# A hybrid decoder step: cached K pages turned in blocks of 32 on VectorE, scored in 4x4 tiles of TensorE

## The chip, the core and the metric

The kernel runs on one core of a Trainium2 chip, as one launch. The metric is device time in microseconds, from the first to the last instruction with what lies around them, and lower is better. Five engines work in parallel, each through its own queue of instructions in program order: TensorE (PE; its weight loads are listed apart as PEld), VectorE (DVE), ScalarE (ACT), GpSimd (POOL) and SyncE (SP), which here issues nearly all transfers. They meet on semaphores: a name after "waits" below is the semaphore that an instruction waits for.

## What is computed

The program is one step of a two-layer decoder trunk for 512 prompt tokens and for 8 sample sequences of 4 new tokens each. A layer has an input projection, an HGRN2 recurrence and differential attention side by side (4 heads each, width 128), an output projection, and a mixture of 16 experts. What matters here is the attention of the sample sequences over a paged cache of 2048 earlier tokens, 16 pages of 128 each, whose numbers come from a page table:

```python
k_past = cache_k[l][page_table].reshape(bd, past_len, DA_HEADS, 2, DA_DK)
v_past = cache_v[l][page_table].reshape(bd, past_len, DA_HEADS, DA_DV)
# diff_attn_core, segments: past, then the new tokens
s = jnp.einsum('bqhcd,bkhcd->bhcqk', q, k).astype(jnp.float32) * scale
scores.append(jnp.where(kpos[None, :] <= qpos[:, None], s, NEG))
p = jax.nn.softmax(jnp.concatenate(scores, axis=-1), axis=-1)
a = p[:, :, 0] - lam * p[:, :, 1]
outs.append(jnp.einsum('bhqk,bkhd->bqhd', a[..., off:off + nk], v.astype(jnp.float32)))
```

Each head has two queries and two keys of 64 (c = 0, 1), so a sequence has 4 heads x 2 maps x 4 tokens = 32 score rows against 2048 keys. A page of K or V is 128 tokens x 512 numbers in fp32, 256 KB; a layer reads 128 pages of each. The sequences are called batches in the code, four pages a quad.

## The kernel before

In each layer the work around the change is one stage of SLOTS = 139 slots. It follows the prompt's attention and ends with the sample's last value product; then come the output projection, the routing and the experts. In every slot each engine's program places what belongs to that slot, so that the slots set the order on each queue: one cached page per slot on PE and ACT, with one item of the HGRN2 recurrence at every slot 5k//3, and the four blocks of the prompt's attention output at slots 2 to 5. The items are the recurrence's levels (PE L901 to L922, DVE L1536 to L1545) and then its blocks; the last eight are the steps of the sample states (POOL L1967 loads a state, DVE L1616 brings it up to date, POOL L1972 and L1974 store it).

A K page arrives with its 128 tokens on the partitions, and the scores need its 512 numbers there. So PE turns each page, four transposes of 128x128 against the identity into one PSUM bank (L744, two banks in alternation), and ACT copies the bank to one of two buffers of a quad (L1311). When a quad is turned, four products of 32 padded query rows with 512 keys follow, one for each head, each on its own 32 columns of the array (L755). A product in fp32 shows as two records in the profile, as x8 for four.

DVE brings the scores of a quad to SBUF with their maximum (L1574). After a batch's four quads come the maximum, four exponentials and one for the new tokens (ACT L1318), then five rounds: p is turned by PE (L777, L779), copied by ACT (L1326, L1328), and multiplied with the quad's V pages (L794, 16 products; L798 for the new tokens). The rows are then divided by their sum (DVE L1597), turned (L806) and written out (L1603, L1604). This happens for each of the eight batches while the next batch's pages are turned.

The transfers of the pages are all issued by SP, at L564: a quad of K, then a quad of V one quad behind. Before each quad SP reads four page numbers (L560) and checks their bounds. K lies in a ring of 8 pages and a load waits for PE's turn of the page it replaces; V lies in a ring of 5 quads and a load waits for the product that used the quad. The pages' room belongs to weights in the other stages, so the first loads of a layer wait for the input projection, and the output projection's weights (L530) wait for the last pages.

## Time and profile before

| | us |
|---|---|
| median of three runs | 1842.38 (1838.37 to 1847.37) |
| profiled execution, its own time | 1847.27 |
| its span, first to last instruction | 1845.6 |
| PE busy in the span | 1664.3 (90%) |
| DVE busy | 550.0 (30%) |
| ACT busy | 485.5 (26%) |
| POOL busy | 161.6 (9%) |

The shares are means over stages that differ much. In the page's 40 slices of the span the DMA share is 0.9 or more in the stages of the experts and of the cached pages, and 0.2 or less in the prompt's attention. The table is thus read as a first look; the stage itself is read in windows, in the groups of its lines and in the timeline.

### The profile page before, as it was taken

Reading aid. Unit: us, or ns where it says so; the run is one execution under the profiler, and the core shown is the slowest. Engines: PE = TensorE matmul, PEld = TensorE weight load, DVE = VectorE, ACT = ScalarE, POOL = GpSimd, SP = SyncE. Lnnn points to the kernel's source line nnn. Section 1 sums busy time; section 2 is a strip of 40 time slices with the busy share of each in tenths; the row PEclk is TensorE's granted clock in tenths of the full one; section 3 lists DMA queues with packets and bytes.
Section 4 is the critical chain, followed back from the end, with each engine's and each line's share of the span. In section 5 each row is a group of like instructions: output and inputs, shape, how many; then the busy total and the mean of one; then the engine's idle time right before and its main releaser. Section 6 shows DMA issues by size and latency. Waiting matters only on the chain. (4 is left out here: it accounts for less than half of the span.)

```text
span 1845.6 us, 32355 instructions
## 1 busy us (share of the span) xinstructions
PE 1664.3 (90%) x12442; PEld 923.6 (50%) x12442; DVE 550.0 (30%) x1522; ACT 485.5 (26%) x1038; POOL 161.6 (9%) x218
## 2 busy tenths in 40 slices
PE   6999998888799999999599999898988999999990
PEld 3457786665445433333244777666744453333330
DVE  2214536434312500000231155453432142000004
ACT  2112335664411011111110233446543110111111
POOL 1000003200100000000200000121010000000002
PEclk9999999999899999999799999999988979999995
DMA  8431009898860699899642200588987309989974
GB/s 259 159 115 46 24 25 330 292 330 284 281 245 32 239 396 411 342 411 411 230 164 81 75 30 24 173 295 309 323 279 276 147 20 385 408 340 411 411 306 168
DMA packets 172364, 437.69 MB, mean 237 GB/s; under 512 B 23921, under 2 KB 23922, under 8 KB 172210
## 3 DMA queue, kind: packets, MB, share of 16 engines
q1 hardware_dynamic: 155650, 377.26, 55.6%
q0 software_dynamic: 16560, 58.34, 8.4%
q8 instruction: 102, 1.67, 0.4%
q14 instruction: 52, 0.43, 0.1%
HBM read 402.91 MB, written 32.64 MB: 236 GB/s over the span
## 5 line engine op out<-in xcount | busy, mean ns | idle before, releaser
L993 PE MATMUL bank<-wslots,heads 128*32 128x512 f32 (+2 forms) x1088 | 266.0, 593 | 8.0 <-DMA hgrn<-in_w_up 4.3
L693 PE MATMUL bank<-xT,wslots 128*128 128x272 f32 x1024 | 241.8, 393 | 1.5 <-ACT heads L1261 0.8
L693 PEld LDWEIGHTS bank<-xT,wslots 128*128 128x128 f32 x1024 | 191.6, 190 | 40.7 <-issue 3.2
L993 PE MATMUL bank<-hgrn,heads 128*32 128x512 f32 (+2 forms) x704 | 182.8, 593 | 0.0
L647 PE MATMUL bank<-wslots,xT 128*128 128x512 f32 x384 | 174.4, 608 | 6.0 <-DMA wslots<-in_w_in 4.3
L744 PE MATMUL bank<-cst,wslots 128*128 128x128 f32 x1024 | 161.8, 286 | 17.5 <-ACT wslots L1311 6.5
L1864 DVE TENSOR_TENSOR temps<-temps,bank 128x512 f32<-128x512 f32 x24 | 16.5, 688 | 449.7 <-PE bank L993 449.7
L993 PEld LDWEIGHTS bank<-wslots,heads 128*32 128x32 f32 (+2 forms) x1088 | 85.2, 127 | 117.5 <-issue 112.9
L1017 PE MATMUL bank<-wslots,temps 128*32 128x512 f32 (+2 forms) x544 | 141.3, 594 | 1.4 <-ACT temps L1352 1.4
L744 PEld LDWEIGHTS bank<-cst,wslots 128*128 128x128 f32 x1024 | 114.3, 143 | 45.5 <-issue 39.2
L647 PEld LDWEIGHTS bank<-wslots,xT 128*128 128x128 f32 x384 | 72.9, 195 | 95.0 <-issue 90.4
L944 PE MATMUL bank<-wslots,xT 128*128 128x512 f32 x256 | 116.3, 615 | 3.8 <-DVE xT L1626 3.8
L1311 ACT ACTIVATE heads<-bank 128x512 f32<-128x512 f32 x128 | 74.5, 594 | 99.6 <-PE bank L744 99.3
L1311 ACT ACTIVATE wslots<-bank 128x512 f32<-128x512 f32 x128 | 75.8, 594 | 82.7 <-PE bank L744 82.7
L993 PEld LDWEIGHTS bank<-hgrn,heads 128*32 128x32 f32 (+2 forms) x704 | 55.2, 122 | 76.9 <-issue 76.9
L944 PEld LDWEIGHTS bank<-wslots,xT 128*128 128x128 f32 x256 | 50.1, 198 | 67.3 <-issue 63.1
L1347 ACT ACTIVATE heads<-bank 128x512 f32<-128x512 f32 x24 | 14.3, 597 | 249.8 <-PE bank L1017 249.8
L1574 DVE TENSOR_SCALAR_CACHE_REDUCE heads<-bank 128x512 f32<-128x512 f32 x64 | 44.2, 691 | 117.9 <-PE bank L755 105.2
L794 PE MATMUL bank<-wslots,heads 128*32 128x128 f32 x2048 | 74.8, 291 | 3.8 <-ACT heads L1326 3.8
L794 PEld LDWEIGHTS bank<-wslots,heads 128*32 128x32 f32 x2048 | 59.8, 117 | 31.8 <-ACT heads L1326 18.0
L1178 ACT ACTIVATE temps<-hid 128x1024 f32<-128x1024 f32 (+1 forms) x25 | 26.4, 1055 | 176.7 <-DVE hid L1848 125.0
L1017 PEld LDWEIGHTS bank<-wslots,temps 128*32 128x32 f32 (+2 forms) x544 | 43.6, 129 | 48.3 <-issue 45.8
(321 smaller groups left out, 2016.3 us busy)
## 6 DMA issues: line engine op xcount, KB each, us to landing
wslots<-in_cache_k SPq DMA_DIRECT2D x256, 256.0 KB, 4.4
wslots<-in_cache_v SPq DMA_DIRECT2D x256, 256.0 KB, 4.5
wslots<-in_w_gate SPq DMA_DIRECT2D x20, 2048.0 KB, 16.1
wslots<-in_w_down SPq DMA_DIRECT2D x20, 2048.0 KB, 15.0
wslots<-in_w_up SPq DMA_DIRECT2D x18, 2048.0 KB, 16.1
wslots<-in_w_in SPq DMA_DIRECT2D x14, 2048.0 KB, 10.3
hgrn<-in_w_up SPq DMA_DIRECT2D x10, 2048.0 KB, 20.3
hgrn<-in_w_gate SPq DMA_DIRECT2D x10, 2048.0 KB, 15.5
```

What stands on the lines that cost most here:

```text
L647: x = mm(bank[2 + m % 2][:, :], xT[:, c, tok(i)], w[:, c, :], start=(c == 0), stop=(c == DC - 1))
L693: x = mm(bank[6 + g % 2][:, 0:HALF], w[:, c, h * P:(h + 1) * P], xT[:, c, half * HALF:(half + 1) * HALF], start=(c == 0), stop=(c == DC - 1))
L744: x = tr(bank[s % 2][:, h * P:(h + 1) * P], kpage[s % NK][:, h, :], ident)
L794: x = mm(bank[5][32 * h:32 * h + 32, 0:HD], ptq[par][:, j, 32 * h:32 * h + 32], vquad[v % NV][:, j, h, :], start=(q == 0 and j == 0), stop ...
L944: x = mm(bank[2 + s][:, :], oT[:, c, tok(i)], w[:, c, :], start=(c == 0), stop=(c == DC - 1))
L993: x = mm(bank[2 + k][a:z, :], xeT[T_ % 2][:, c, a:z], weights((what, l, e), DC)[:, c, :], start=(c == 0), stop=(c == DC - 1))
L1017: x = mm(bank[5 + n][a:z, :], hT[T_ % 2][:, c, a:z], weights(("down", l, e), 4)[:, c, n * WB:(n + 1) * WB], start=(c == 0), stop=(c == 3))
L1178: link(A(junk[0:r, :], hid[0:r, i, :], ACT.Square, accum_out=ssq[0:r, i:i + 1]))
L1311: A(ktb[s // 4 % 2][:, s % 4].rearrange("p h n -> p (h n)"), bank[s % 2][:, :], ACT.Copy).then_inc(kt_ok, 1)
L1347: A(yt[b][:, 0:WB], bank[5][:, :], ACT.Copy).then_inc(y_ok, 1)
L1574: tell(V.tensor_scalar(scr[G_ % 6], bank[2][:, :], 1.0, None, ALU.mult, ALU.max, accum_out=mx5[:, g % 4:g % 4 + 1]), sq_ok)
L1864: link(V.tensor_tensor(hgt, silu[T_ % 2], bank[3][:, :], ALU.mult), hg_ok)
```

## The change

K pages are no longer turned whole. DVE transposes two pages with one instruction in place, by blocks of 32x32 (`turn_pages`, 64 a layer); after that each block has 32 of the 512 numbers on its partitions. The scores of a batch then run over all 16 pages at once: `batch_scores` has four steps d, one for each block of 32 numbers of a head, and each step has 16 products of 32x32 against 512 keys, one for each row group a and head h of the array. The four steps add up in four PSUM banks, one for each row group. Four batches share these banks: each has eight of the 32 rows (the padded queries put it there), so four batches share one round of score output, exponentials, turns of p and division (two groups a layer instead of eight batches).

K lies in three units of eight pages in slots 1 to 3, of which 24 pages are loaded ahead of the stage, and V in three quads. SP follows a list (`page_order`): 24 K pages and a V quad ahead, two V quads after the last projection weights; then four K quads after the scores of each batch, with V quads sorted between by their slots. The bounds checks of the page numbers are gone, and their read follows the wait. The slots' tables are new: scores at 13n to 13n + 3, the DVE's turns between, values for the first four batches at slots 51 to 88 and for the second four at 103 to 133. The first eight turns stand ahead of the division of the prompt's attention output on DVE. The first level of the recurrence on PE waits for that output's copy (`od_ok`). Smaller edits: the causal mask of the prompt's attention is made of `tri` by one operation, queries are spread to four row groups by 16 copies (`spread_queries`), and the logits are cleared after the stage.

```diff
+GB = 4
+GROUPS = DB // GB
+UNIT = 8
+NU = 3
+SCORE_BANKS = (0, 1, 2, 4)
...
-        kpage = [w_a[:, 4096 + 512 * s:4096 + 512 * (s + 1)].rearrange("p (h n) -> p h n", h=H) for s in range(8)]
-        vquad = [w_a[:, o:o + 2048].rearrange("p (j h n) -> p j h n", j=4, h=H) for o in (8192, 10240, 12288, 0, 2048)]
-        NK, NV = len(kpage), len(vquad)
+        kring = w_a[:, 4096:16384].rearrange("p (u g x) -> p u g x", u=NU, g=UNIT)
+        vquad = [a.rearrange("p (j h n) -> p j h n", j=4, h=H) for a in (t_a[:, 4096:6144], w_a[:, 0:2048], w_a[:, 2048:4096])]
+        NV = len(vquad)
...
-        ktb = [a.rearrange("p (j h n) -> p j h n", j=4, h=H) for a in (w_a[:, 14336:16384], t_a[:, 0:2048])]
-        scr = [t_a[:, 2048 + 512 * i:2560 + 512 * i] for i in range(6)]
-        ptq = [t_a[:, 5120 + 512 * i:5632 + 512 * i].rearrange("p (j n) -> p j n", j=4) for i in range(2)]
+        scr = t_a[:, 0:2048]
+        scr_out = scr.rearrange("p (g a k) -> p a g k", g=NPG, a=4)
+        ptq = t_a[:, 2048:4096].rearrange("p (g n) -> p g n", g=NPG)
+        on = t_a[:, 2048:2560]
...
-        def turns(b):
-            return (3, 5, 7, 9, 11) if b < DB - 1 else (3, 4, 5, 6, 7)
+        SLOTS = DB * NPG + 11
+        SCORES = [13 * n for n in range(DB)]
+        TURN_AT = {SCORES[n - 1] + d: 8 * n + x for n in range(1, DB) for x, d in enumerate((1, 3, 5, 7, 9, 10, 11, 12))}
+        SUM_UP = [SCORES[GB * g + GB - 1] + 4 for g in range(GROUPS)]
+        VALUES = [SUM_UP[0] + 8 + 5 * k // 2 for k in range(16)] + [SUM_UP[1] + 8 + 2 * k for k in range(16)]
+        NEW_AT = (8, SUM_UP[1] - 2)
+        ROWS_AT = (VALUES[15] + 2, VALUES[31] + 1)
...
+        def page_order():
+            late = [(SCORES[(q // 2 - NU) // 2] + 4, 0, q) for q in range(2 * NU, NQ)]
+            late += [(VALUES[v - NV] + 1, 1, v) for v in range(NV, NQ)]
+            early = [(0, 0, q) for q in range(2 * NU)] + [(0, 1, v) for v in range(NV)]
+            return early + sorted(late)
...
+                    for _, kind, q in page_order():
+                        if kind == 0:
+                            n, first_page = unit_pages(q // 2)
+                            slot, _count = k_fill(l, q)
+                            if q < 2 * NU:
+                                sp.wait_ge(*last_use(("in", l, 3 + q // 2)))
                             else:
-                                sp.wait_ge(pv_ps, vn(v - NV) + 1)
+                                sp.wait_ge(sq_ps, DB * l + (q // 2 - NU) // 2 + 1)
+                            ids = four_pages((NPG * n + first_page) // 4 + q % 2)
                             for j in range(4):
-                                load_page(previous[j], vquad[v % NV][:, j], t_in["cache_v"], vl[v % NV])
-                    sp.wait_ge(kt_ps, (l + 1) * DB * NPG)
+                                load_page(ids[j], kring[:, unit_of(q // 2), 4 * (q % 2) + j, :], t_in["cache_k"], kl[slot])
+                        else:
+                            if q == 0:
+                                sp.wait_ge(pa_pv, 16 * (l + 1))
+                                sp.wait_ge(st_v, 16 * NT * (l + 1))
+                            elif q < NV:
+                                sp.wait_ge(*last_use(("in", l, 6)))
+                            else:
+                                sp.wait_ge(pv_ps, vn(l, q - NV))
+                            ids = four_pages(q)
+                            for j in range(4):
+                                load_page(ids[j], vquad[q % NV][:, j].rearrange("p h n -> p (h n)"), t_in["cache_v"], vl[q % NV])
...
-            def page_turn(l, s):
-                g = l * DB * NPG + s
-                pe.wait_ge(kl[s % NK], 16 * (int(s % NK < NT) + l * (DB * NPG // NK) + s // NK + 1))
-                if g >= 2:
-                    pe.wait_ge(kt_ok, g - 1)
+            def batch_scores(l, n, d):
+                i, B = n % GB, l * DB + n
+                if d == 0:
+                    pe.wait_ge(kt_ok, 8 * B + 8)
+                    pe.wait_ge(qp_ok, B + 1)
+                    if i == 0:
+                        pe.wait_ge(sq_ok, 4 * (B // GB))
+                u, z = sorted((unit_of(2 * n), unit_of(2 * n + 1)))
                 for h in range(H):
-                    x = tr(bank[s % 2][:, h * P:(h + 1) * P], kpage[s % NK][:, h, :], ident)
-                x.then_inc(kt_ps, 1)
-            def quad_scores(l, g):
-                G_ = l * NQ + g
-                Q = qn(G_)
-                pe.wait_ge(kt_ok, 4 * G_ + 4)
-                pe.wait_ge(qz_ok, G_ // 4 + 1)
-                pe.wait_ge(sq_ok, Q)
+                    q0 = 24 - 8 * i + 32 * (H * d + h)
+                    c0 = h * HD + 32 * d
+                    for a in range(4):
+                        r = slice(32 * a, 32 * a + 32)
+                        x = mm(bank[SCORE_BANKS[a]][32 * h:32 * h + 32, :], qp[r, q0:q0 + 32], kring[r, u:z + 1:z - u, :, c0:c0 + 32],
+                               start=(i == 0 and d == 0), stop=(i == GB - 1 and d == 3))
+                if d == 3:
+                    x.then_inc(sq_ps, 1)
...
+            def new_values(l, g):
+                G = GROUPS * l + g
+                pe.wait_ge(pt_ok, 5 * G + 5)
+                for h in range(H):
+                    x = mm(bank[5][32 * h:32 * h + 32, :], ptn[0:NS, 32 * h:32 * h + 32],
+                           vtok[0:NS, PT, h * HD:(h + 1) * HD].unsqueeze(1).to_broadcast([NS, GB, HD]), start=True, stop=False)
+                x.then_inc(pv_ps, 1)
+            def quad_values(l, v):
+                i, q = v % 16 // 4, v % 4
+                slot, filled = v_fill(l, v)
+                pe.wait_ge(vl[slot], filled)
+                for j in range(4):
                     for h in range(H):
+                        x = mm(bank[5][32 * h:32 * h + 32, i * HD:(i + 1) * HD], ptq[:, 4 * q + j, 32 * h:32 * h + 32], vquad[slot][:, j, h, :],
+                               start=False, stop=(v % 16 == 15 and j == 3))
...
+                if m == 0 and h == 0:
+                    pe.wait_ge(od_ok, PT * (l + 1))
...
-                    if s < DB * NPG:
-                        page_turn(l, s)
-                    if s % 4 == 0 and 1 <= s // 4 <= NQ:
-                        quad_scores(l, s // 4 - 1)
...
+                    for n in range(DB):
+                        if 0 <= s - SCORES[n] < 4:
+                            batch_scores(l, n, s - SCORES[n])
+                    for g in range(GROUPS):
+                        if s == NEW_AT[g]:
+                            new_scores(l, g)
+                        if 2 <= s - SUM_UP[g] < 7:
+                            turn_p(l, g, s - SUM_UP[g] - 2)
+                        if s - SUM_UP[g] == 7:
+                            new_values(l, g)
+                        if s == ROWS_AT[g] + 1:
+                            turn_o(l, g)
+                    if s in VALUES:
+                        quad_values(l, VALUES.index(s))
...
-                        act.wait_ge(kt_ps, l * DB * NPG + s + 1)
-                        if G_ >= 2:
-                            act.wait_ge(sq_ps, qn(G_ - 2) + 1)
-                        A(ktb[s // 4 % 2][:, s % 4].rearrange("p h n -> p (h n)"), bank[s % 2][:, :], ACT.Copy).then_inc(kt_ok, 1)
...
+            def turn_pages(l, x):
+                q = x // 2
+                slot, filled = k_fill(l, q)
+                dve.wait_ge(kl[slot], filled)
+                two = kring[:, unit_of(q // 2), 4 * (q % 2) + 2 * (x % 2):4 * (q % 2) + 2 * (x % 2) + 2, :].rearrange("p g n -> p (g n)")
+                tell(V.transpose(two, two), kt_ok)
...
             def scores_out(l, g):
...
+                G = GROUPS * l + g
+                dve.wait_ge(sq_ps, GB * (G + 1))
+                if G:
+                    dve.wait_ge(pt_ps, 6 * (G - 1) + 4)
+                for a in range(4):
+                    tell(V.tensor_scalar(scr_out[:, a], bank[SCORE_BANKS[a]][:, :].rearrange("p (g k) -> p g k", k=32), 1.0, None, ALU.mult, ALU.max,
+                                         accum_out=mx5[:, a:a + 1]), sq_ok)
...
                 link(x, od_sq)
+                queries(l, 0)
+                new_queries(l, 0)
+                for x in range(8):
+                    turn_pages(l, x)
...
+                    if s in TURN_AT:
+                        turn_pages(l, TURN_AT[s])
+                    if s - 5 in SCORES and SCORES.index(s - 5) + 1 < DB:
+                        queries(l, SCORES.index(s - 5) + 1)
```

On PE, in the first batches, before (L744 turns pages, L755 scores, L901 and L910 are a level of the recurrence):

```order
L755 MATMUL bank<-wslots,smalls 32x512 [waits s_scores_ready,s_queries,page_t_ready]
L755 MATMUL bank<-wslots,smalls 32x512 x3
L744 MATMUL bank<-cst,wslots 128x128 [waits page_t_ready,x_tile_then_k_page_loaded5]
L744 MATMUL bank<-cst,wslots 128x128 x3
L901 MATMUL bank<-hgrn 32x32 [waits h_level_taken,h_queries]
L901 MATMUL bank<-hgrn 32x32 x15
L910 MATMUL bank<-hgrn 32x32
L744 MATMUL bank<-cst,wslots 128x128 [waits page_t_ready,x_tile_then_k_page_loaded6]
L744 MATMUL bank<-cst,wslots 128x128 x3
L744 MATMUL bank<-cst,wslots 128x128 [waits page_t_ready,x_tile_then_k_page_loaded7]
L744 MATMUL bank<-cst,wslots 128x128 x3
```

And now at the second and third batch (L792 scores, L943 the same level):

```order
L952 MATMUL bank<-hgrn 32x32
L792 MATMUL bank<-wslots,smalls 32x512 [waits s_queries,page_blocks_turned]
L792 MATMUL bank<-wslots,smalls 32x512 x15
L943 MATMUL bank<-hgrn 32x32 [waits h_level_taken,h_keys,h_queries]
L943 MATMUL bank<-hgrn 32x32 x15
L792 MATMUL bank<-wslots,smalls 32x512 x32
L943 MATMUL bank<-hgrn 32x32 [waits h_keys,h_queries]
L943 MATMUL bank<-hgrn 32x32 x15
L792 MATMUL bank<-wslots,smalls 32x512 x16
L943 MATMUL bank<-hgrn 32x32 [waits h_keys,h_queries]
L943 MATMUL bank<-hgrn 32x32 x15
```

The page turns are gone between the levels, and the scores stand in bursts of 64 products a batch; only the first product of a burst has waits, for the turned blocks and the queries, and the level behind it in the queue stands behind those waits too.

On DVE, about the same place before (L1544 and L1545 are the level's two operations, L1536 and L1537 its masks, L1574 the score output, L1565 padded queries):

```order
L1544 TENSOR_TENSOR hgrn<-hgrn 128x136x2 [waits h_queries,h_level_psum]
L1545 TENSOR_TENSOR hgrn<-hgrn 128x136 [waits dve_steps]
L1574 TENSOR_SCALAR heads,smalls<-bank 128x512 [waits s_scores_psum]
L1565 COPY smalls<-smalls 64x4x4 [waits s_scores_psum]
L1565 COPY smalls<-smalls 64x4x4
L1536 COPY_PREDICATED temps<-cst,bank 128x32 [waits h_level_taken,h_level_psum,s_queries]
L1537 COPY_PREDICATED temps<-cst,bank 128x512
```

And now (L1576 and L1577 are the level's, L1568 and L1569 the masks, L1605 the queries, L1623 the transposes):

```order
L1623 STREAM_TRANSPOSE wslots<-wslots 128x1024 [waits x_tile_then_k_quad_loaded3]
L1605 COPY smalls<-smalls 128x8x4 [waits s_scores_psum]
L1605 COPY smalls<-smalls 128x8x4
L1568 COPY_PREDICATED temps<-cst,bank 128x32 [waits h_level_taken,h_level_psum,s_queries]
L1569 COPY_PREDICATED temps<-cst,bank 128x512
L1576 TENSOR_TENSOR hgrn<-hgrn 128x272 [waits h_queries,h_level_taken]
L1577 TENSOR_TENSOR hgrn<-hgrn 128x272 [waits dve_steps]
L1623 STREAM_TRANSPOSE wslots<-wslots 128x1024 [waits x_tile_then_k_quad_loaded3]
```

Between the pairs of a level and the queries now stand transposes, each of which waits for a quad of K to land, and the level's next operations stand behind it.

On SP, in the steady run of the pages before (each ISA row ahead of a K page is its wait and address):

```order
L564 ISA [waits page_t_psum]
L564 DMA wslots<-in_cache_k 128x512
L564 DMA wslots<-in_cache_v 128x512 [waits s_values_psum]
L564 DMA wslots<-in_cache_v 128x512 x3
L560 TENSOR_LOAD smalls
L560 ISA x8
L564 ISA [waits page_t_psum]
```

And now, where K quad 16 of the layer follows on K quad 15:

```order
L601 DMA wslots<-in_cache_k 128x512
L601 ISA
L601 DMA wslots<-in_cache_k 128x512
L596 TENSOR_LOAD smalls [waits s_scores_psum]
L601 ISA
L601 DMA wslots<-in_cache_k 128x512
```

A wait for each page has become a wait for each quad on a whole batch's scores, the eight checks of the numbers are gone, and V has moved out of the pairs.

## Rows read from the trace of the kernel before

**Rows 1.** Timeline of PE, stage edges (start, length, engine, line, operation, count)

```profile
270.25 0.66 PE L744 MATMUL bank<-cst,wslots 128*128 128x128 f32 x4 [0.49 <-ACT hgrn L1278]
...
513.24 0.42 PE L798 MATMUL bank<-heads 32*32 32x128 f32 x8
```

**Rows 2.** Windows: length; busy PE, PEld, DVE, ACT, POOL; clock; DMA share; GB/s

```profile
270.00:514.00 244.00, 210.85 (x3208) 145.72 (x3208) 104.22 (x306) 133.80 (x280) 40.11 (x51) 0.94 0.86 291
1172.00:1416.00 244.00, 210.19 (x3209) 144.68 (x3209) 104.92 (x306) 133.69 (x280) 40.06 (x51) 0.94 0.86 291
```

**Rows 3.** PE's groups of lines, 270 to 517 (busy us, mean ns, idle before)

```profile
L744 PE MATMUL bank<-cst,wslots 128*128 128x128 f32 x512 | 81.1, 286 | 7.5 <-ACT wslots L1311 3.6 <-ACT heads L1311 3.1 <-ACT hgrn L1278 0.5
L794 PE MATMUL bank<-wslots,heads 128*32 128x128 f32 x1024 | 37.6, 292 | 1.9 <-ACT heads L1326 1.9
```

**Rows 4.** Waits of SP's queue, 275 to 500 (total us, times, longest)

```profile
SPq L564 <- PE bank L794: 27.0, 8, 6.2
SPq L564 <- PE bank L744: 16.9, 9, 4.7
```

**Rows 5.** Windows, a stretch late in the stage

```profile
488.60:496.60 8.00, 7.45 (x115) 4.76 (x114) 2.15 (x9) 5.26 (x11) 0.76 (x1) 1.00 1.03 370
```

**Rows 6.** DVE's groups by shape, whole span

```profile
L1409 DVE SCALAR_TENSOR_TENSOR hid<-hgrn,smalls,hid 128x1024 f32<-128x1024 f32 x16 | 20.6, 1284 | 58.1 <-DMA hgrn<-y_scratch,smalls 57.6
L1394 DVE TENSOR_SCALAR temps<-hid,smalls 128x1024 f32<-128x1024 f32 x16 | 12.1, 754 | 0.6
```

**Rows 7.** DVE's groups of lines in the stage, 270 to 514

```profile
L1574 DVE TENSOR_SCALAR_CACHE_REDUCE heads<-bank 128x512 f32<-128x512 f32 x32 | 22.1, 691 | 57.9 <-PE bank L755 51.8 <-issue 4.9 <-DVE hgrn L1616 1.0
L1545 DVE TENSOR_TENSOR hgrn<-hgrn 128x272 f32<-128x272 f32 (+6 forms) x28 | 15.3, 548 | 1.0
L1544 DVE TENSOR_TENSOR hgrn<-hgrn 128x256 f32<-128x256 f32 (+1 forms) x28 | 12.9, 461 | 16.7 <-PE bank L907 6.5 <-PE bank L901 4.2 <-PE bank L910 4.2
L1537 DVE COPY_PREDICATED temps<-cst,bank 128x512 f32<-128x512 uint32 x5 | 3.7, 739 | 2.1 <-PE bank L901 2.1
L1831 DVE TENSOR_SCALAR xT<-bank,smalls 128x512 f32<-128x512 f32 x4 | 3.0, 750 | 1.2 <-PE bank L734 1.0
L1539 DVE TENSOR_TENSOR hgrn<-hgrn 128x544 f32<-128x544 f32 x4 | 2.9, 726 | 0.2
L1565 DVE COPY smalls<-smalls 64x16 f32<-64x16 f32 x14 | 2.3, 167 | 0.1
```

**Rows 8.** Timeline of DVE ahead of the stage (idle before in brackets)

```profile
260.92 0.25 DVE L1806 RECIPROCAL smalls<-smalls 128x16 f32<-128x16 f32 x1 [8.66 <-ACT smalls L1282]
261.21 2.87 DVE L1809 TENSOR_TENSOR temps<-temps,smalls 128x512 f32<-128x512 f32 x4
```

**Rows 9.** Timeline of PE, three places of matmuls that share the array

```profile
216.52 1.13 PE L704 MATMUL bank<-heads 64*128 64x512 f32 x4
...
254.70 15.06 PE L693 MATMUL bank<-xT,wslots 128*128 128x272 f32 x65
...
275.11 1.07 PE L755 MATMUL bank<-wslots,smalls 128*32 128x512 f32 x8
```

**Rows 10.** The page, DMA issues (KB each, us to landing)

```profile
wslots<-in_cache_v SPq DMA_DIRECT2D x256, 256.0 KB, 4.5
```

**Rows 11.** Timeline, the last batch's softmax

```profile
499.05 1.06 PE L755 MATMUL bank<-heads,smalls 128*32 128x512 f32 x8 [0.69 <-ACT heads L1311]
...
504.52 0.57 ACT L1326 ACTIVATE heads<-bank 128x512 f32<-128x512 f32 x1
```

**Rows 12.** Timeline of DVE, sample states, step one and step eight

```profile
453.44 1.12 DVE L1616 SCALAR_TENSOR_TENSOR hgrn<-hgrn,bank 128x128 f32<-128x128 f32 x4 [3.96 <-PE bank L922]
...
487.54 1.12 DVE L1616 SCALAR_TENSOR_TENSOR hgrn<-hgrn,bank 128x128 f32<-128x128 f32 x4 [2.81 <-PE bank L922]
```

**Rows 13.** Window at 407.3, columns as above, and PE's row in it

```profile
407.30:409.30 2.00, 1.98 (x16) 0.65 (x20) 0.00 (x0) 1.98 (x4) 0.00 (x0) 0.50 1.02 391
...
407.32 1.94 PE L755 MATMUL bank<-wslots,smalls 128*32 128x512 f32 x8 [1.17 <-ACT wslots L1311]
```

300 lines of the change are left out of this document (138 added, 162 removed).

## Prediction

> **What bounds the kernel now.** I read the busy time by stretches first, because a share of the whole span mixes projection, attention and experts. The change lies in one stage of each layer, from the first page turn to the last value product [rows 1]: 270.25 to 513.24 + 0.42 = 513.66, so 243.4 us, and the windows of the second layer show the same stage to within 1% [rows 2]. Expect to see there TensorE busy 210.9 of 244 us, VectorE 104, ScalarE 134, DMA at 0.86 share and 291 GB/s. TensorE is the fullest. The groups of its lines say with what: the 512 page turns alone take 81.1 us, more than the cached values (37.6) [rows 3]. The waits of SP's own queue come third: 27.0 us for a value product to free a V buffer, 16.9 us for a page turn to free a K buffer [rows 4]. So the loads follow TensorE's pace. They are not the limit yet, but near: in a stretch without waits 370 GB/s go through [rows 5], and one quad (four pages, 4 x 256 KB = 1.049 MB) needs 2.83 us at that rate. 64 quads of a layer are 181 us. That floor, not TensorE, is what the changed stage runs into.
>
> **The change, part by part** (one layer; time 0 is slot 0).
>
> *Removed.* 81.1 us of page turns on TensorE, their 128 copies on ScalarE, six of eight rounds of exponentials and turns of p. None of this counts by itself: what is late next sets the time. SP issues lose their bounds checks; SP was not the last there, so zero, unless its 16-page waits were issue time, at most a few us.
>
> *Added: 64 transposes of 128x1024 on VectorE.* No row shows a VectorE transpose. The rows from both sides: 1024 columns cost 0.754 us in a one-input operation and 1.284 us in a two-input one [rows 6]; 128x544 with two inputs takes 0.726 and 128x512 0.691 [rows 7]. A transpose in place that moves one element per lane at the slope of these, 1.04 ns, is 1.23 us. I take 1.23, near the slow row; for the ends 0.754, and twice my value, 2.46, if blocks cost a second pass. The Trainium skill ("Vector Engine (DVE) Microarchitecture Reference", section 3.8 on transpose, 5.2 on costs) gives one element per cycle per lane and about 75 ns of fixed cost; an estimate from that page is 1.14 us, and the sum below would end about 6 us lower. No row here shows the operation, so the page cannot be tested yet.
>
> *Stage A, slots 0 to 51: VectorE.* Scores of batch 4 need the turns of batches 1 to 4, 32 x 1.23 = 39.4. Between them in the same queue stand the recurrence's levels: 15.3 + 12.9 + 3.7 + 2.9 = 34.8, less the last level (4 pairs of 0.548 + 0.461, 4.0), 30.8 [rows 7]; four scalings of the attention output, 3.0 (L1831); one group's score output, four at 0.691, with about 1 for readouts and maximum (by the short row of 0.167), 3.8; 12 query copies at 0.167, 2.0. Sum 79.0, with the short copies between them 80. Each of four score bursts makes a level's TensorE work late, and VectorE behind it, by about 1.5: 6. So batch 4's turns are done at 86, its scores (below, 5.5) at 92. Before, VectorE was busy 43% of the stage [rows 2]; in this stretch it should now be nearly full.
>
> *The first 8 turns and the 24 K pages loaded ahead* cost nothing: VectorE waits 8.66 us for ScalarE's roots just there and 2.87 us of scaling follow [rows 8]; the prompt attention has no other DMA. If that cover were gone it is 8 x 1.23 = 9.8.
>
> *16 tiles of 32x32 at once.* A 512-column pass on one row and column group should take two records: 65 records of 272 columns in 15.06 us are 0.232 each, so 0.437 a pass, 0.874 serial. Four column tiles take 1.07 together [rows 9], not 3.5; two row tiles of 64x512 took 1.13, not 1.75. Both directions overlap, separately. That all 16 overlap no row shows: I take 1.07 per step of 16 (below: 3.7 if the row groups go one after another), 4.3 a batch with 1.2 for waiting on the last turn, 5.5. The Trainium skill ("TensorE: Matmul & The Clock Gate", Part 3, packing small matmuls) has a 4x4 packing with this shape measured at 10.6, not 16 times. By it a step is 16 x 0.874 / 10.6 = 1.32, 1.0 more a batch, some 6 us a layer in all, and the median 1826 instead of 1814.
>
> *Stage B: DMA.* Between the scores of batch 4 and of batch 7, SP issues K quads 22 to 31 and V quads 5 to 15, 21 in one queue, and each K quad waits for scores, each V quad for values. At 2.83 us that is 59.4; about 1 for SP to read its page numbers (an estimate), 4.5 for the last landing [rows 10], 5.5 for scores: batch 7's scores at 92 + 70 = +162. The wait of a V quad behind a K quad on SP is an order of its own: if values are late, K is.
>
> *Stage C: the second softmax and the tail.* In the kernel before the way from the last scores to the first usable p takes 499.05 + 1.06 to 504.52 + 0.57, 5.0 us [rows 11]. Now three more score outputs (2.1), four more rounds of turn and copy (0.66 and 0.57 with two handovers, 1.45 each: 5.8) and the new-token values (3) stand ahead: 16 us, V16 at +178. In these slots stands also the chain of sample states: eight steps, from 453.44 to 487.54 for seven, 4.9 each [rows 12], each through a state load. Alone, without waits by pages, I take 30 us for it: +210. Behind it on TensorE lie five quads; 5.5 for the first and 4 x 2.83, values of 1.1: +228. The output turns of four batches cost 1.2 more than before.
>
> *The sum.* 243.4 - 228 - 1.2 = 14 us a layer, 28 in two. The profiled execution took 1847.3 (1845.6 of it the span): 1819. It lies 4.9 above the median 1842.4; taken over, 1814.
>
> **The rivals.**
>
> *Quick transposes (faster).* If a transpose runs like the one-input row, 0.754 [rows 6], stage A loses 32 x 0.48 = 15 a layer: 1784. For it: the transpose has one input, as that row has. Against: the row writes what it reads in the same order, and blocks of 32 do not; no row shows such a pattern at that pace.
>
> *Cold TensorE (the other side).* TensorE loses 81 us of dense work per layer; stage A leaves it waiting on VectorE. The granted clock here does fall: 0.50 (of 2.4 GHz, so 1.2) in the window at 407.3, after a wait of 1.17 us, and four score tiles take 1.94 there for 1.07 [rows 13]. At 1.2 GHz a batch of scores takes 4 x 0.88 = 3.5 more. Eight batches do not all lie on the path, five do: 17.5; with the softmax rounds 3.5 and the tail 2.3, 23 a layer. Half of that gives 1837 (same), all of it 1860. It decides against the change from 14 us a layer, that is from about 60% of this stage at the low level. For it: such gaps exist even in the dense kernel. Against: HGRN levels and values still fill the gaps, and the mean here is 0.94 [rows 2].
>
> *Costly transposes.* 2.46 each: 32 x 1.23 + 8 = 47 a layer, 1908. Against: no 1024-column row is over 1.284.
>
> *The row groups go one after another*, so the change does not do what it says: a step of 3.7 instead of 1.07, 2.6 x 4 x 5 = 42 and 9 of stage C and batch 0, 51 a layer, 1916. Against: two row tiles do overlap [rows 9].
>
> **How the numbers follow.** Forecast 0.43 (own range 1795 to 1833, 9.5 us a layer to either side: down if the bursts' waits, 6, vanish and the state chain is 3.5 shorter; up if the cover of the first 8 turns, 9.8, is gone), of which 0.03 lie within 0.5%. Quick transposes 0.20, cold 0.18 (0.10 within, 0.08 slower), costly 0.11, serial 0.08. 0.5% is 9.2 us and about what a measurement of this kernel can tell from no change: faster below 1833, slower above 1852. Faster: 0.40 + 0.20 = 0.60; same 0.03 + 0.10 = 0.13; slower 0.08 + 0.11 + 0.08 = 0.27. The range leaves out half of the serial case, some of the costly and the far half of the quick one: 1775 to 1895.
>
> **What would show it.** Transposes at a mean of 1.2 us and VectorE over 90% busy in the first 90 us; 0.75 or 2.4 decides the first rival or the third. A step of 16 tiles at about 1.1 us against 3.7. DMA share near 1.0 between +92 and +160, SP waiting for scores and hardly for values. TensorE's clock in the first 90 us: near 1.0, or under 0.7 for the cold case. The sample-state chain 30 us long, and a stage of 228 us in both layers, with the output projection's last weights right behind it. I am wrong if the DMA share stays under 0.9 in stage B (then issue or waits, not the rate, set it), or if the tail after the last scores is over 66 us.

## The result

The change makes the kernel slower: 1902.2 us (median of 4 runs, 1899.0 to 1908.5) against 1841.5 before, a ratio of 1.033 with an interval of 1.029 to 1.037. The forecast was 1814, with a range up to 1895. The profiled span is 1899.0 us, 53.4 above the one before; the two stages take nearly all of it.

Both operations that the forecast had to guess came out near the guess. These are two groups of the page after the change (busy us, mean ns, idle before and what ended it):

```profile
L1623 DVE STREAM_TRANSPOSE wslots<-wslots 128x1024 f32<-128x1024 f32 x128 | 154.2, 1227 | 9.7 <-DMA wslots<-in_cache_k 8.9
L792 PE MATMUL bank<-wslots,smalls 32*32 32x512 f32 x2048 | 92.6, 751 | 55.8 <-DVE wslots L1623 54.7
```

A transpose takes 1.227 us; 1.23 was taken. A step of 16 score products is the first row below, 1.15 us where 1.07 was taken; over the whole stage the mean is 1.45 (92.6 us by 64 steps), as many steps run at a lower granted clock. So most of the loss is elsewhere. The stage's milestones are read from TensorE's timeline of the first layer: the first scores, the last step of batch 4's and of batch 7's scores, the first and the last value product of the second group:

```profile
268.76 1.15 PE L792 MATMUL bank<-wslots,smalls 32*32 32x512 f32 x32 [0.49 <-ACT hgrn L1320]
...
366.60 2.35 PE L792 MATMUL bank<-wslots,smalls 32*32 32x512 f32 x64
...
460.19 1.14 PE L792 MATMUL bank<-wslots,smalls 32*32 32x512 f32 x32
...
479.51 3.64 PE L836 MATMUL bank<-wslots,heads 128*32 128x128 f32 x64
...
537.75 1.93 PE L836 MATMUL bank<-wslots,heads 128*32 128x128 f32 x32 [1.00 <-DMA wslots<-in_cache_v]
```

| us after 268.76 | forecast | measured | stretch, forecast | stretch, measured |
|---|---|---|---|---|
| batch 4 scored | 92 | 100.2 | 92 | 100.2 |
| batch 7 scored | 162 | 192.6 | 70 | 92.4 |
| first value of the second group | 178 | 210.8 | 16 | 18.2 |
| last value | 228 | 270.9 | 50 | 60.2 |

The stage of before took 243.4 [rows 1], so a layer loses 27.5 where 14 were to be won. The second layer repeats it (batch 4 at +100.0, batch 7 at +192.4). Of the 43 us between forecast and measurement 22 lie in the second stretch. The same columns as [rows 2], in three pieces:

```profile
270.00:350.00 80.00, 39.84 (x1318) 20.09 (x1318) 63.64 (x106) 7.83 (x17) 18.96 (x23) 0.72 0.61 211
350.00:450.00 100.00, 60.37 (x1105) 39.65 (x1103) 50.06 (x76) 11.83 (x21) 10.19 (x14) 0.73 0.85 299
450.00:540.00 90.00, 58.82 (x811) 35.22 (x810) 26.28 (x84) 10.43 (x22) 10.52 (x14) 0.70 0.61 212
```

No engine is full any more: TensorE 40 of 80, 60 of 100 and 59 of 90 us, VectorE 64, 50 and 26, DMA shares 0.61, 0.85, 0.61. Before, TensorE had 210.9 of 244. This is a stage that waits, one engine for the other; and the granted clock is 0.72 in the mean instead of 0.94. The waits of SP's queue (245 to 545), which answer to [rows 4], name the place:

```profile
SPq L596 <- PE bank L836: 77.2, 15, 32.6
SPq L596 <- PE bank L792: 38.8, 5, 12.5
```

SP waits 77 us for value products to free V buffers (32.6 of them in one wait, for the second softmax) and 39 for scores. In between TensorE waits for V (its timeline):

```profile
387.94 1.93 PE L836 MATMUL bank<-wslots,heads 128*32 128x128 f32 x32 [13.54 <-DMA wslots<-in_cache_v]
...
419.95 1.94 PE L836 MATMUL bank<-wslots,heads 128*32 128x128 f32 x32 [10.85 <-DMA wslots<-in_cache_v]
...
444.53 1.93 PE L836 MATMUL bank<-heads 128*32 128x128 f32 x32 [8.59 <-DMA heads<-in_cache_v]
```

SP's issues ahead of the first of them:

```profile
366.59 2.85 SPq L601 DMA_DIRECT2D wslots<-in_cache_v  x4
369.95 9.42 SPq L601 DMA_DIRECT2D wslots<-in_cache_k  x16
379.89 1.88 SPq L601 DMA_DIRECT2D wslots<-in_cache_v  x4
```

After batch 4's scores, which end at 368.95, SP issues four K quads in a row, and only then V quad 5. Its buffer was free at 370.57, when the product of V quad 2 ended; the K quads hold its issue until 379.89, 9.3 of the 13.5 us for which TensorE waits. TensorE stands in front of that value product; the next batch's scores are behind it in its queue, and the next four K quads are behind those scores in SP's list. The two queues take turns.

### The profile page after: what moved, and what is told of

Its sections match the earlier page's. It is cut to its first block and busy times, and to the rows that moved or that the text cites. A ratio compares the mean times of both kernels' runs of the same rounds, so it can differ in the third digit from the quotient of the medians.

```text
span 1899.0 us, 31107 instructions
## 1 busy us (share of the span) xinstructions
PE 1561.0 (82%) x12558; PEld 823.0 (43%) x12558; DVE 651.5 (34%) x1500; ACT 278.5 (15%) x598; POOL 160.4 (8%) x218
## 5 line engine op out<-in xcount | busy, mean ns | idle before, releaser
L1623 DVE STREAM_TRANSPOSE wslots<-wslots 128x1024 f32<-128x1024 f32 x128 | 154.2, 1227 | 9.7 <-DMA wslots<-in_cache_k 8.9
L792 PE MATMUL bank<-wslots,smalls 32*32 32x512 f32 x2048 | 92.6, 751 | 55.8 <-DVE wslots L1623 54.7
L836 PE MATMUL bank<-wslots,heads 128*32 128x128 f32 x1344 | 61.9, 344 | 62.8 <-DMA wslots<-in_cache_v 62.8
L836 PEld LDWEIGHTS bank<-wslots,heads 128*32 128x32 f32 x1344 | 47.4, 139 | 80.4 <-DMA wslots<-in_cache_v 67.1
L1997 POOL TENSOR_TENSOR hgrn<-hgrn 128x256 f32<-128x256 f32 (+1 forms) x56 | 46.7, 834 | 136.6 <-PE bank L943 61.2
L792 PEld LDWEIGHTS bank<-wslots,smalls 32*32 32x32 f32 x2048 | 23.4, 116 | 79.6 <-DVE wslots L1623 56.6
L2002 POOL DMA_DIRECT2D y_scratch<-heads x24 | 13.7, 572 | 509.2 <-ACT heads L1383 509.2
L1059 PE MATMUL bank<-xT,temps 128*32 128x512 f32 (+1 forms) x192 | 56.6, 594 | 0.0
L1059 PE MATMUL bank<-hgrn,temps 128*32 128x512 f32 (+1 forms) x256 | 56.4, 593 | 0.0
```

The costliest lines, as they stand in the source:

```text
L792: x = mm(bank[SCORE_BANKS[a]][32 * h:32 * h + 32, :], qp[r, q0:q0 + 32], kring[r, u:z + 1:z - u, :, c0:c0 + 32], start=(i == 0 and d == 0) ...
L836: x = mm(bank[5][32 * h:32 * h + 32, i * HD:(i + 1) * HD], ptq[:, 4 * q + j, 32 * h:32 * h + 32], vquad[slot][:, j, h, :], start=False, st ...
L1059: x = mm(bank[5 + n][a:z, :], hT[T_ % 2][:, c, a:z], weights(("down", l, e), 4)[:, c, n * WB:(n + 1) * WB], start=(c == 0), stop=(c == 3))
L1623: tell(V.transpose(two, two), kt_ok)
L1997: link(G.tensor_tensor(k[:, :, 0, :], k[:, :, 0, :], f[:, :, 1, 0:1].to_broadcast([P, j, b]), ALU.mult), hK)
```

## The experiments

Three theories were set against each other: **one list** (V behind four K quads in SP's list, scores behind values in TensorE's queue), **ring and states** (the tail is set by a V ring of three quads and by the chain of sample states), and **cold TensorE**, the rival of the prediction. All edits are to the changed kernel unless said otherwise. The table has the milestones of the first layer, read as above (us after the first scores), and the run; where no ratio is given below, it is a single run, timed beside before on the same chip. Runs of one version lie up to 11 us apart (e11: 1847.3 to 1858.3), so two single runs that differ by less are told apart only by milestones that agree in both layers.

| run | batch 4 scored | batch 7 scored | last value | run, us |
|---|---|---|---|---|
| the change | 100.2 | 192.6 | 270.9 | 1902.2 |
| e1_kv_mixed | 98.1 | 179.1 | 257.0 | 1875.8 |
| e2_busy_fill | 98.2 | 190.8 | 273.0 | 1910.2 |
| e3_no_turns | 90.3 | 177.1 | 254.9 | 1865.3 |
| e4_three_v_quads | 100.8 | 169.8 | 226.2 | 1808.9 |
| e5_states_early | 100.3 | 206.2 | 274.1 | 1906.2 |
| e6_v_in_k_ring | 101.6 | 195.1 | 269.6 | 1898.1 |
| e8_batch4_first | 97.1 | 184.6 | 262.1 | 1882.2 |
| e9_all | 98.0 | 179.5 | 254.7 | 1865.9 |
| e10_values_first | 96.7 | 178.7 | 251.4 | 1861.5 |
| e11_states_in_softmax | 97.2 | 181.2 | 247.0 | 1851.4 |
| e12_busy_tail | 95.9 | 178.4 | 248.0 | 1854.1 |
| e13_busy_tail_states | 95.8 | 178.5 | 252.4 | 1866.6 |
| e14_early_turns | 94.5 | 177.3 | 248.6 | 1863.4 |
| e15_k_once | 98.3 | 166.2 | 243.8 | 1845.7 |
| e16_no_fill_in_values | 94.8 | 177.9 | 245.4 | 1854.3 |
| before | | | 243.4 | 1840.6 to 1843.3 |

### K and V mixed in SP's list

```diff
-            late = [(SCORES[(q // 2 - NU) // 2] + 4, 0, q) for q in range(2 * NU, NQ)]
+            late = [(SCORES[(q // 2 - NU) // 2] + 4 + 3 * ((q + 2) % 4) * int(q >= 22), 0, q) for q in range(2 * NU, NQ)]
```

> The changed kernel with one edit: in the second half of the K loads, SP takes a V quad after each K quad instead of four K quads in a row. Theory 'one list' (V quads queued behind four K quads land late, TensorE waits for them with the next scores behind it): the waits of 13.5, 10.9 and 8.6 us for V before a value product fall under 5 each, the last scores come at about +177 us instead of +192.6, and the run takes about 1870 us instead of 1902. Rival 'cold TensorE' (the loss is the lower granted clock): no change within 8 us. Rival 'ring and states' (the loss is in the tail): the last scores may come earlier, the stage's end does not, within 8 us.

1875.8 us. Batch 7's scores come 13.5 us earlier and the last value 13.9; the tail behind them is unchanged (77.9 after 78.3). TensorE's waits between 350 and 450 us, first of the change, then of this run:

```profile
PE bank L836 <- DMA wslots<-in_cache_v: 24.4, 2, 13.5
PE bank L836 <- DMA heads<-in_cache_v: 9.6, 2, 8.6
```

```profile
PE bank L792 <- DVE wslots L1623: 9.8, 3, 3.8
PE bank L836 <- DMA wslots<-in_cache_v: 8.8, 3, 4.7
PE bank L836 <- DMA heads<-in_cache_v: 6.5, 2, 4.8
```

The waits for V in this stretch fall from 34.0 to 15.3 us, the longest from 13.5 to 4.8. One line of a list was worth 26 us of the run; the second layer repeats the gain of its stage (12.4 us). The part "one list" stands, and the tail is a part of its own.

### TensorE kept busy

```diff
+            def keep_busy():
+                for h in range(H):
+                    mm(bank[0][32 * h:32 * h + 24, :], qp[:, 32:56], cst[:, 256:256 + WB], start=False, stop=False)
...
+                    if (4 <= s < 39 or 56 <= s < 91) and s % 13 > 3:
+                        keep_busy()
```

> The changed kernel with products by zero weights added to the open score banks, four column tiles in each slot that has no scores, slots 4 to 38 and 56 to 90. Nothing else moves. Theory 'cold TensorE': the granted clock in the first 90 us rises from 0.67 to over 0.9, bursts of 7.4 us shrink to about 5.5, batch 4's scores end at about +88 instead of +100, and the run takes about 1875 us. Theory 'one list' and 'VectorE sets the first stretch': the clock rises, but the last scores and the end move by less than 5 us a layer; the run stays over 1890, or gets slower by the added products where TensorE does not wait (up to 10 us a layer).

1910.2 us. The window of the first 80 us:

```profile
270.00:350.00 80.00, 62.21 (x1580) 26.86 (x1552) 64.27 (x107) 9.31 (x20) 19.08 (x24) 0.88 0.65 218
```

The mean clock rose from 0.72 to 0.88, VectorE's busy time is the same, and batch 4 came 2.0 us earlier, batch 7 1.8; in the second layer neither did. That is no gain net of the products' own time, but it is not yet the price of the clock, because most bursts of scores in the first stretch did not speed up. The first half of batch 3's, in the change and in this run:

```profile
334.34 4.08 PE L792 MATMUL bank<-wslots,smalls 32*32 32x512 f32 x64 [7.11 <-DVE wslots L1623]
```

```profile
332.62 4.08 PE L792 MATMUL bank<-wslots,smalls 32*32 32x512 f32 x64 [3.39 <-DVE wslots L1629]
```

Of the four bursts only batch 1's got shorter, 7.36 to 5.38 us, as much as batch 4 came earlier; the expected 5.5 was not reached in the others. Four bursts of 5.38 would be 8 us less in a layer. In the second stretch the three bursts did get shorter, by 4.5 us together, and the stretch did not (92.7); there some of the added products themselves stand ahead of scores. So the low clock is there, as the rival said, and keeping TensorE busy does not win back the loss; what the level of the bursts costs by itself, 8 and 4.5 us in these two stretches if all of it is on the path, stays open.

### What the transposes, V and K cost by themselves

Three runs leave one thing out each: the transposes, the V loads after three quads, the K loads after 24 pages.

```diff
-                tell(V.transpose(two, two), kt_ok)
+                tell(V.tensor_copy(two[:, 0:1], two[:, 1:2]), kt_ok)
```

> Left out: the 64 transposes of a layer; a copy of one column takes the place of each, so that all waits stay. Theory 'VectorE sets the first stretch': batch 4's scores end at +60 to +78 instead of +100 (32 x 1.23 = 39 us leave the queue; the softmax of the first group and the K loads, 16 quads of 2.83, remain), the run falls to about 1850. Rival 'the softmax on TensorE's queue ahead of batch 4': the scores of batch 3 come early, but batch 4's end follows them by the same 27 us as now. If V and K in one list set the second stretch: batch 4 to batch 7 stays within 8 us of 92.

Batch 3's scores end at 64.0 instead of 73.1, batch 4's at 90.3 instead of 100.2: 32 transposes less 32 short copies are 32 x (1.227 - 0.146), some 35 us of VectorE's queue, and 10 of them were on the path. The range that VectorE's queue alone had given, +60 to +78, is missed by 12; the rival's sign is there, batch 4 still follows batch 3 by 26 us. Nor is the softmax the only next limit: batch 3 itself came 9 us earlier where its 24 turns would free 26, and VectorE waited 11.0 us for K pages instead. The second stretch takes 86.8, within 8 of 92.

```diff
-            return early + sorted(late)
+            return early + sorted(x for x in late if x[1] == 0)
...
-                slot, filled = v_fill(l, v)
-                pe.wait_ge(vl[slot], filled)
+                slot = v % NV
+                pe.wait_ge(vl[slot], 64 * (l + 1))
```

> Left out: all V loads of a layer after the first three quads; the value products run on these again and again. Theory 'one list': TensorE has no wait for V, scores of batch 7 come at about +160 (K alone, 10 quads after batch 4, 28 us, and VectorE's work), the tail is the softmax and the state chain, about 45 us: some 50 us a layer less, about 1800. Rival 'cold TensorE': the waits go but products still run at the low level, at most 20 us a layer less, about 1860. If the chain of sample states is what ends the tail, the tail stays over 55 us even here.

1808.9 us, and the stage ends 44.7 us earlier. The second stretch is 69.0 instead of 92.4. The tail after the last scores is 56.4 instead of 78.3, although the state steps have the same slots. So the V loads are worth 22 us of the tail. What is left is over the 55 at which the chain of states was to be what ends it; its first and its last step are these:

```profile
463.46 1.25 DVE L1676 SCALAR_TENSOR_TENSOR hgrn<-hgrn,bank 128x128 f32<-128x128 f32 x4 [4.91 <-PE bank L964]
...
489.14 1.12 DVE L1676 SCALAR_TENSOR_TENSOR hgrn<-hgrn,bank 128x128 f32<-128x128 f32 x4 [2.59 <-PE bank L964]
```

The steps take 3.7 us each here and, as the section on the tail shows, 4.7 with the V loads. TensorE's waits for the state loads are 1.3 us instead of 7.5.

```diff
-            return slot, 16 * int(slot < NT) + 64 * (per * l + w // NU + 1)
+            return slot, 16 * int(slot < NT) + 64 * (l + 1)
...
-            return early + sorted(late)
+            return early + sorted(x for x in late if x[1] == 1)
...
+                if q >= 2 * NU:
+                    dve.wait_ge(sq_ps, DB * l + (q // 2 - NU) // 2 + 1)
```

> The changed kernel; left out: all K loads of a layer after the first 24 pages. The transposes and the waits for the scores that would free a unit stay, so only SP's issue, the rate and the landing are gone. Theory 'VectorE sets the first stretch': batch 4's scores still end at +95 to +100. Rival 'the loop scores, K load, landing, last turns, scores sets it' (the second half of a batch's K can load only after the scores before): the four batches come every 15 to 18 us instead of 21 to 23 and batch 4 ends at +82 to +88. In the second stretch V no longer stands behind K: batch 4 to batch 7 takes 65 to 75 us instead of 92, the run about 1840.

1845.7 us. The first stretch hardly moves (98.3), so the K loop does not set it. The second takes 67.9. With K alone 69.0, with V alone 67.9, with both in one list 92.4. TensorE's waits between 350 and 450, first without V, then without K:

```profile
PE bank L792 <- DVE wslots L1623: 19.4, 3, 7.5
PE bank L815 <- ACT heads L1354: 5.8, 1, 5.8
```

```profile
PE bank L792 <- DVE wslots L1625: 9.5, 3, 4.0
PE bank L815 <- ACT heads L1354: 5.8, 1, 5.8
```

So about 68 us are what the engines take between the two milestones when no load of the other kind is in the way.

VectorE's work alone does not set the first stretch either. Its first 90 us in the changed kernel, and what VectorE waited for (268 to 360):

```profile
268.76:358.76 90.00, 47.12 (x1401) 23.63 (x1401) 69.20 (x113) 11.84 (x24) 20.58 (x25) 0.70 0.61 212
```

```profile
DVE xT L1896 <- PE bank L775: 8.9, 1, 8.9
DVE hgrn L1576 <- PE bank L943: 5.9, 4, 2.3
DVE hgrn L1576 <- PE bank L952: 3.7, 2, 2.8
DVE hgrn L1576 <- PE bank L946: 3.3, 3, 2.8
```

It is busy 69 of 90 us. It waits for TensorE, for the turned attention output and for products of the recurrence's levels.

### The first softmax ahead of batch 4

TensorE's timeline between batch 3's last scores and batch 4's first in the changed kernel:

```profile
340.76 1.14 PE L792 MATMUL bank<-wslots,smalls 32*32 32x512 f32 x32
...
346.71 1.12 PE L815 MATMUL bank<-cst,heads 128*128 128x128 f32 x4 [4.39 <-ACT heads L1354]
...
357.21 1.93 PE L825 MATMUL bank<-heads,smalls 32*32 32x512 f32 x8 [0.36 <-ACT smalls L1362]
...
361.91 3.14 PE L792 MATMUL bank<-wslots,smalls 32*32 32x512 f32 x64
```

It waits for the exponentials and turns p before batch 4, 20 us in all. The edit puts the five turns behind batch 4's scores:

```diff
+        TURN_P = (53, SUM_UP[1] + 2)
-        VALUES = [SUM_UP[0] + 8 + 5 * k // 2 for k in range(16)] + [SUM_UP[1] + 8 + 2 * k for k in range(16)]
+        VALUES = [59 + 2 * k for k in range(16)] + [SUM_UP[1] + 8 + 2 * k for k in range(16)]
...
-                        if 2 <= s - SUM_UP[g] < 7:
-                            turn_p(l, g, s - SUM_UP[g] - 2)
+                        if 0 <= s - TURN_P[g] < 5:
+                            turn_p(l, g, s - TURN_P[g])
...
```

> The changed kernel with other slots alone: the turns of p of the first group stand behind batch 4's scores on TensorE instead of ahead of them, values at every second slot from 59. Theory 'the first softmax holds up batch 4' (TensorE's queue waits 20 us for it with batch 4's scores behind): batch 4's scores end at +84 to +92 instead of +100. Theory 'VectorE sets the first stretch': not earlier than +96. For the run: as the second stretch hangs on V quads, which now come later, about 1895 to 1905.

```profile
359.51 3.61 PE L793 MATMUL bank<-wslots,smalls 32*32 32x512 f32 x64 [6.93 <-DVE wslots L1624]
```

Batch 4 now waits 6.93 us for its last transposes instead, and is scored at 97.1: VectorE's end of this stretch is only 3 us before the softmax's, as the second theory had said (not earlier than +96). The run is 20 us shorter all the same, where 1895 to 1905 was expected, since the second stretch fell to 87.5 and the tail by 0.8; SP's list is sorted by these slots, so V and K stand in it in another order, and how much of the gain is due to that I did not separate.

### The tail

In the 35 us after V quad 18 is issued the DMA is nearly idle; the window, and SP's issues around it:

```profile
447.00:482.00 35.00, 23.74 (x276) 15.03 (x278) 15.61 (x40) 10.13 (x21) 0.00 (x0) 0.70 0.13 42
```

```profile
446.99 1.88 SPq L601 DMA_DIRECT2D heads<-in_cache_v  x4
481.97 5.19 SPq L601 DMA_DIRECT2D wslots<-in_cache_v  x8
```

The ring of three quads is full and nothing can free it before the second softmax is done. After that 13 quads come through it, with the state steps between the products (VectorE's timeline, step one and eight, as [rows 12]):

```profile
485.05 1.25 DVE L1676 SCALAR_TENSOR_TENSOR hgrn<-hgrn,bank 128x128 f32<-128x128 f32 x4 [5.14 <-PE bank L964]
...
518.23 1.12 DVE L1676 SCALAR_TENSOR_TENSOR hgrn<-hgrn,bank 128x128 f32<-128x128 f32 x4 [2.18 <-PE bank L964]
```

33.2 us for seven steps, 4.7 each, hardly less than the 4.9 of before. Two edits tried one cause each.

```diff
-            k = (3 * s + 4) // 5
-            return items[k] if 0 <= k < len(items) and 5 * k // 3 == s else (None, 0, 0)
+            k = (3 * s + 4) // 5 if s < 60 else s - 24
+            return items[k] if 0 <= k < len(items) and (s >= 60 or 5 * k // 3 == s) else (None, 0, 0)
```

> The changed kernel with the recurrence's items from number 36 on in every slot instead of three in five, so that the sample states' eight steps stand at slots 88 to 95, about the second softmax, and not between the last value products. Theory 'ring and states' (the tail after the last scores is long because steps that wait for state loads stand between products that free the V ring): the tail falls from 78 us after the last scores to about 60, the run to about 1870. If the ring of three V quads alone sets it: 13 quads at some 4 us, the tail changes by less than 6 us. Theory 'one list': the second stretch (batch 4 to batch 7) is not shorter by this, within 5 us.

The tail fell by 10.4 us, to 67.9 where about 60 was expected, and the second stretch grew by 13.5: the time was moved from one stretch to another. No gain, 1906.2.

```diff
+        vquad += [w_a[:, o:o + 2048].rearrange("p (j h n) -> p j h n", j=4, h=H) for o in (8192, 10240, 12288, 14336)]
...
+                            elif 19 <= q < 23:
+                                sp.wait_ge(sq_ps, DB * l + (7 if q < 21 else 8))
...
```

> The changed kernel with one edit: V quads 19 to 22 are loaded into the two K units that are free after the scores of batches 6 and 7, so that seven instead of three quads are there when the second softmax is done. Theory 'DMA is idle in the second softmax because the V ring is full' (35 us without a load, 447 to 482): four quads, 4 x 2.83 = 11 us, leave the tail; the end of the stage comes 8 to 12 us earlier, the run takes about 1880. Rival 'the chain of sample states sets the tail': less than 4 us a layer. Rival 'cold TensorE': less than 4 us.

The tail fell by 3.8 us, to 74.5, and by 6.7 in the second layer, and the stage ended 1.3 and 5.1 us earlier: a miss for "the ring is full", which asked for 8 to 12. Four quads more were there, and most of the tail stayed.

> The three edits together: K and V mixed in SP's list, V quads 19 to 22 in the free K units, batch 4's scores ahead of the first softmax. If each of the three waits is a cause of its own: 13 + 10 + up to 8 us a layer, 1902 - 62 = 1840, the same as before the change. If they are one and the same wait: not below 1865.

1865.9 us (ratio 1.013, 1.010 to 1.017), far from 1840 and within 1 us of 1865, the bound for one and the same wait. The three edits are worth 26, 20 and 4 alone and 36 together. The windows of the second stretch show a limit that they have in common, first of e1, then of this run:

```profile
368.00:449.00 81.00, 55.73 (x995) 36.66 (x980) 43.25 (x72) 8.14 (x14) 6.14 (x9) 0.79 0.91 332
```

```profile
366.00:448.00 82.00, 59.14 (x1078) 38.90 (x1063) 43.01 (x71) 9.60 (x17) 6.38 (x9) 0.85 1.00 363
```

With the order mended the DMA is full: share 1.00 and 363 GB/s, the rate of [rows 5]. At 2.83 us a quad these 82 us are 29 quads, and 28 go through. This is the floor of the forecast, reached at last; e10, e11 and e16 have the same 361 to 366 GB/s there. With the DMA full, another order of K and V within this stretch has nothing left to win; fewer loads in it might, and no run here tried that. Two more edits to the slots on top of it:

```diff
-        VALUES = [59 + 2 * k for k in range(16)] + [SUM_UP[1] + 8 + 2 * k for k in range(16)]
+        VALUES = [59 + 2 * k for k in range(16)] + [SUM_UP[1] + 8 + k if k < 7 else SUM_UP[1] + 2 + 2 * k for k in range(16)]
```

> The run of the three edits together, and beside them other slots alone for the last value products: the seven quads that are there when the second softmax is done run in seven slots in a row (103 to 109) instead of every second one, so fewer steps of the sample states stand between them. Theory 'the tail is slots in which state steps hold the products that free the V ring': the V loads start up to 15 us earlier and the stage's end comes 6 to 12 us a layer earlier, about 1848. Rival 'the chain of states itself is the tail' (34 us, wherever its steps stand): less than 4 us a layer, about 1862.

```diff
+            k = (3 * s + 4) // 5 if s < 60 else 36 + (3 * (s - 60) + 3) // 4
+            at = 5 * k // 3 if k < 36 else 60 + 4 * (k - 36) // 3
```

> As the run with the value products first, and the recurrence's items from number 36 on at every slot 4k/3 instead of 5k/3, so that the state steps begin at slot 97, beside the second softmax, on whose exponentials TensorE waits. If the chain of states is the tail, up to 12 us a layer less than that run, about 1835. If what is moved ahead makes the second stretch longer, as with the items in every slot (13.6 us there), no gain.

1861.5, and then 1851.4 us (ratio 1.007, 1.005 to 1.009). Running the products first ends the stage 3.3 and 3.1 us earlier in the two layers, which is what the rival had foretold (under 4, about 1862). With the state steps beside the exponentials on which TensorE waits anyway the tail is 65.8 us after 72.7, and the stage ends 4.4 and 6.2 us earlier, about half of what was expected. So where the steps stand matters more than when the products run. The order of loads and slots, with four quads in K's room, has taken back 51 of the 61 us.

### The clock in the tail, and what fillers cost

```diff
+            def keep_busy(n):
+                for _ in range(n):
+                    mm(bank[0][:, :], ident, cst[:, 256:256 + WB], start=True, stop=True)
...
+                            keep_busy(5)
...
+                    if 104 <= s < 128:
+                        keep_busy(1)
```

> As the run with the value products first, and products that nobody reads: five ahead of the second softmax's first turn and one in each slot from 104 to 127. Theory 'cold TensorE' for the tail: the granted clock there rises from 0.66 to over 0.85, value products fall from 1.94 to 1.1 us, and the end comes 5 us a layer earlier. Rival 'loads and state steps set the tail': the clock rises and the end stays within 3 us a layer.

The window 446 to 525 without and with the products:

```profile
446.00:525.00 79.00, 51.21 (x691) 30.82 (x690) 22.74 (x79) 9.90 (x21) 10.56 (x14) 0.69 0.73 246
```

```profile
446.00:525.00 79.00, 67.69 (x750) 32.94 (x719) 24.00 (x80) 9.64 (x21) 10.52 (x14) 0.95 0.75 254
```

The clock rose from 0.69 to 0.95. The end came 3.4 us earlier, between the 5 and the 3 that the theories asked for, and the single runs differ by 7.3. In the second layer it came 3.7 earlier, but there batch 7's scores, ahead of which no product was added, already came 4.0 earlier, and the tail behind them did not get shorter. So a price of the low level in the tail of about 3 us a layer is possible and not shown.

> The run with the state steps beside the second softmax, and beside it the unread products of the busy tail. If the low clock costs the tail what the busy tail showed (7 us), the median is about 1844, within 0.5% of before; if the two edits fill the same gaps, about 1850.

1866.6 us (ratio 1.013, 1.011 to 1.015), 15 more than without the products: a miss on both sides. The timeline offers a reason; L823 is the unread product:

```profile
503.92 1.08 PE L854 MATMUL bank<-heads 128*32 128x128 f32 x32
504.94 1.98 PE L823 MATMUL bank<-cst 128*128 128x512 f32 x4
506.85 1.08 PE L854 MATMUL bank<-wslots,heads 128*32 128x128 f32 x32
```

Two of them in two slots, 1.98 us, between any two value products: with the state steps gone from there, the unread products themselves set the pace, 2.93 us a quad.

```diff
+                for x in range(8, 12):
+                    turn_pages(l, x)
                 dve.wait_ge(st_v, 16 * NT * (l + 1))
```

> As the run before it, and the four turns of batch 1 whose pages are there already stand ahead of slot 0, where VectorE waits 8.9 us for the turned attention output. Theory 'VectorE sets the first stretch': up to 4 x 1.23 = 4.9 us a layer less, median about 1836. Rival 'the K loop sets it': under 2 us a layer.

1863.4 us (ratio 1.011, 1.008 to 1.014), not 1836. For 4.9 us that left VectorE's queue batch 4 comes 1.3 us earlier in the first layer and 0.9 later in the second, so the theory that VectorE's queue sets the first stretch fails here. The rival's number, under 2 us, is met, but e15 speaks against its reason, the K loop. What the stretch hangs on besides, the waits between VectorE and TensorE shown above among it, no run separates.

> All edits to the order together (K and V mixed, V quads 19 to 22 in free K units, batch 4's scores ahead of the first softmax, value products first, state steps beside the second softmax, four turns ahead of slot 0), and of the unread products only the five ahead of the second softmax's first turn; those between the value products are gone, since there they took 1.85 us of every 2.93. If these were why the last two runs came out 12 to 15 us above the run without them, the median is 1842 to 1850, within 0.5% of before. If the early turns or the five products cost something, above 1855.

1854.3 us (ratio 1.007, 1.005 to 1.009), between the two expected ranges. Without the products between the values 9 of the 12 us are back; the first layer's stage is 245.4, within 2 us of before. It is no better than e11, and no version found here beats the kernel before.

### The bounds checks

The kernel before, with the checks of the page numbers left out:

```diff
-                            ptab[0:1, 4 * g:4 * g + 4], engines=(mybir.EngineType.SP,), min_val=0, max_val=t_in["cache_k"].shape[1] - 1)[1]
+                            ptab[0:1, 4 * g:4 * g + 4], engines=(mybir.EngineType.SP,), min_val=0, max_val=t_in["cache_k"].shape[1] - 1,
+                            skip_runtime_bounds_check_because="the page table names pages of the cache")[1]
```

> The kernel before with one part of the change alone: the bounds checks of the page numbers are gone. Theory 'the loads follow TensorE's pace there': within 0.5% of before (1833 to 1850). Rival 'SP's issue was the limit of that stage' (64 x 8 instructions a stage): 1% or more faster, under 1823.

1838.6 us, ratio 0.998 (0.997 to 1.000). SP's issue was not what that stage waited for.

## Why the prediction was wrong

- **What bounds the kernel before**: right that the issue on SP was not the limit (b1 moved nothing); that the loads followed TensorE's pace rests on the waits of [rows 4]. Wrong in the last sentence, that the rate of 370 GB/s is what the changed stage runs into: it moved 211, 299 and 212 GB/s in its three pieces. Only with the order mended does one stretch reach it (e9, 363).
- **Transposes, 1.23 us**: right, 1.227, and partly by luck. The 1.04 ns a column that the working calls the slope of its rows is not theirs: 0.726 at 544 columns and 1.284 at 1024 give 1.16. Both rivals that hung on the price, quick and costly, fall with it.
- **Stage A, 92**: 100.2. The total was near for the wrong reason. VectorE was to be over 90% busy and was busy 69 of 90 us. Its last turn for batch 4 ended at +93 instead of +86: the work was priced 8 us too high (80, measured 72), the waits 15 too low (6, measured 21). What the step also left out is TensorE's queue: V quad 0 has slot 51 and batch 4's scores have slot 52, so the whole first softmax stood ahead of them. It is worth 3 us here, since without it VectorE's turns still end at +89.5 (e8). That 32 transposes are all on the path was wrong: without them 10 us went, and K pages and the softmax were next.
- **16 tiles at once, 1.07 us a step**: 1.15 at a granted clock of 1.00, in 4.6 of the stage's first 6.1 us; the row groups do not go one after another. A batch, though, took 7.0 to 9.3 us for 5.5, with the lower clock and other products between.
- **Stage B, 70**: 92.4, and the step that decided. The sum priced the DMA (21 quads at 2.83) and let everything else hide behind it. The runs without V and without K show 69.0 and 67.9 us for the engines' own chain, somewhat longer than the 59.4 of transfers that were priced. Two chains hide behind each other only if they run at the same time; with four K quads ahead of each V quad in one list, and scores behind values in one queue, they took turns. The prediction had the sentence ("if values are late, K is") and gave it no price; mixing the list took back 13.5 us in the first layer. Its sign for this came as written: a DMA share of 0.82 in the stretch, under 0.9, and SP waited 77 us for values and 39 for scores, where the prediction had it wait hardly for values.
- **Stage C and the tail, 16 and 50**: 18.2 and 60.2. The first state step began 5.5 us after the first value, where 2 was left; the chain was sized at 30 us and took 34, and the quads behind it took 20 instead of 18. That is the 10 us of the tail. "Without waits by pages" was the weak premise: without V loads the same chain took 27 (e4), and TensorE waited 1.3 us for its state loads instead of 7.5. The nearly idle DMA in the softmax (share 0.13 over 35 us) was not in the working; four quads loaded ahead, in K's room, gave back 1.3 and 5.1 us at the stage's end. The second sign of being wrong came too: 78.3 us after the last scores, for 66.
- **The cover of the first eight turns**: right. They ran in VectorE's wait, and the first scores came 1.5 us before the first page turn of before [rows 1].
- **Cold TensorE, 0.18**: its premise came true, 0.72 where [rows 2] has 0.94. Of its price of 23 us a layer no run shows more than 2 in the first stretch, none in the second and some 3 in the tail, but most bursts of the first stretch were not brought to the upper level, and in the second the added products stood in the way themselves, so that 8 and 4.5 us stay possible there. Mixing the list took 26 us from the run with no product added, so the clock is not the main cause.
- **The other side**: the rivals on the slow side were prices of single operations and of the clock. The one that came, two queues waiting for each other, was in none of them, so the range ended 7 us short.

What stays open: what sets the first stretch beside the order of TensorE's queue, what the clock costs by itself, and the last 10 us between the best order and before. In e11 the stages are 247.0 and 244.4 us long, 3.6 and 1.1 more than before, and the steps behind the last value are 6.2 us to the output projection for 4.3, twice. With the DMA full in e11's second stretch (361 GB/s), room is left where it is not: its share is 0.59 in the first stretch and 0.74 in the tail.

## What to carry to other kernels

When a change makes the fullest engine lighter, write down for each remaining stretch what the next two limits are and whether they can run at the same time in the queues as written; limits of similar size in one list may take turns instead of hiding each other. Once the order is mended, look for the floor again: here the transfer rate that the forecast had named came out only then. Larger batches need buffers for a whole batch, and what they take from another ring can come back as idle transfers where a result of the whole batch is awaited; four quads loaded ahead of it alone gained little here. A list of loads should alternate by when its users come in their queue, and a low granted clock should be priced by a run that keeps the engine busy, before it is called a cause; and that run is to be read at the products on the path, since a higher mean may come from the added products alone.

## What the hardware showed that was not expected

- Sixteen 32x32 tiles of 512 columns took 1.15 us together at a granted clock of 1.00, where 0.874 each in a row would be 14.0: a factor of 12.2. The packing measured in the Trainium skill ("TensorE: Matmul & The Clock Gate", Part 3) is 10.6 times; the measurement here decides for this form, and the estimate by that page, 1.32, was too high.
- The transpose of 128x1024 on VectorE, in place, takes 1.227 us, 1.20 ns a column; of the rows with 1024 columns that is near the 1.284 with two inputs and far from the 0.754 with one [rows 6]. The estimate by the Trainium skill ("Vector Engine (DVE) Microarchitecture Reference", sections 3.8 and 5.2) was 1.14; the measurement lies 0.09 us above it.
- After a wait the first step of a batch took 2.02 us, for 1.15 in batch 0; TensorE's timeline at batches 1 and 2 of the change:

```profile
290.43 2.02 PE L792 MATMUL bank<-wslots,smalls 32*32 32x512 f32 x32 [9.11 <-DVE wslots L1623]
...
313.48 2.02 PE L792 MATMUL bank<-wslots,smalls 32*32 32x512 f32 x32 [4.08 <-DVE wslots L1623]
```

The granted clock in both is 0.50, the lower level (1.2 of 2.4 GHz), after waits of 9.11 and 4.08 us:

```profile
290.43:292.40 1.97, 1.97 (x35) 0.31 (x35) 0.00 (x0) 0.00 (x0) 0.00 (x0) 0.50 0.05 15
313.48:315.40 1.92, 1.92 (x32) 0.28 (x32) 1.51 (x4) 0.00 (x0) 0.00 (x0) 0.50 0.01 5
```

It is 0.87 us for the first step; the whole bursts of batches 1 to 4 took 7.0 to 7.7 us.
